# x and the histories ahead of the modulation weights, the modulation split between the projections, the norm rows made during out_b

## The reference

```
mod = silu(c) @ w_ada + b_ada                      # (9, 6*1024): shift1, scale1, gate1, shift2, scale2, gate2
u = x * (1 + scale1) + shift1
b_g, c_g, xa, xp, g_a, g_b = split(u @ w_in)       # w_in: 1024 x 4096
zc = concat(conv_hist, c_g * xa);  conv = sum_j conv_w[j] * zc[:, j:j+T]
y_a = (b_g * conv) @ w_out_a
diff = multiscale_pool(concat(pool_hist, xp))
y_b = (einsum(diff, w_pool) * ls_pool) @ w_out_b
merged = sigmoid(g_a) * y_a + sigmoid(g_b) * y_b
h = layer_norm(ALPHA * x + gate1 * (merged @ w_o), ln1_g, ln1_b)
v = h * (1 + scale2) + shift2
f = moe_ffn(v)                                     # router, top 4 of 32, SwiGLU experts
y = layer_norm(ALPHA * h + gate2 * f, ln2_g, ln2_b)
```

## Time and profile before

| | |
|---|---|
| three runs | 1304.96, 1297.54, 1305.26 us; median 1304.96 |
| the profiled execution | 1306.29 us, its span 1304.5 us |
| PE busy | 1202.6 us (92%) |
| DVE, ACT, POOL busy | 550.4, 226.6, 160.6 us |
| DMA | 466.54 MB, mean 358 GB/s over the span |

### The profile page before, as it was taken

The page is one execution under the profiler, slowest core; times in us unless marked ns, Lnnn a source line. Parts: engine busy times, 40 slices in busy tenths (PEclk is TensorE's granted clock), DMA queues, the critical chain, the costliest instruction groups (busy, mean ns, idle before and its releaser), DMA issues.

```text
span 1304.5 us, 17407 instructions
## 1 busy us (share of the span) xinstructions
PE 1202.6 (92%) x6170; PEld 520.2 (40%) x6171; DVE 550.4 (42%) x1044; ACT 226.6 (17%) x350; POOL 160.6 (12%) x97
## 2 busy tenths in 40 slices
PE   4899999979899999999899999999999999999990
PEld 0599964433333333333333333333333333333330
DVE  0517825874434333433334333443343433334337
ACT  0233210133112111111111111111111111111110
POOL 0367443024400000000000000000000000000023
PEclk8799999969899999999999999999999999999995
DMA  9744499649999999999996999998899999699951
GB/s 335 261 153 173 193 310 369 245 183 400 394 425 428 426 427 427 426 426 425 425 426 255 427 425 426 426 428 356 333 426 428 427 427 426 263 425 426 426 237 40
DMA packets 54789, 466.54 MB, mean 358 GB/s; under 512 B 5516, under 2 KB 5548, under 8 KB 18642
## 3 DMA queue, kind: packets, MB, share of 16 engines
q1 hardware_dynamic: 52817, 460.32, 85.9%
q0 software_dynamic: 1952, 5.97, 1.4%
HBM read 464.42 MB, written 1.85 MB: 357 GB/s over the span
## 4 chain that ended last, share of the span: by engine, by line
PE 60%; DMA 27%; DVE 9%; SPq 2%; ACT 1%; issue 1%; POOL 0%; DVEq 0%; ACTq 0%
PE bank L870 28%; DMA ring<-in_w_up 21%; PE bank L904 13%; PE bank L647 8%; PE bank L844 3%; DMA mod_rows<-parts_home 3%; DMA hx<-in_x_sample 2%; PE bank L767 2%; PE bank L633 2%; DVE front L1354 1%; PE bank L895 1%; ACT front L1038 1%; DVE front L1348 1%; PE bank L862 1%; DVE front L1345 1%
## 5 line engine op out<-in xcount | busy, mean ns | idle before, releaser
L870 PE MATMUL bank<-ring,front 128*64 128x512 f32 x2240 | 505.9, 597 | 20.3 <-DMA ring<-in_w_up 20.3
L870 PEld LDWEIGHTS bank<-ring,front 128*64 128x64 f32 x2240 | 153.5, 137 | 314.7 <-issue 269.8
L904 PE MATMUL bank<-ring,front 128*64 128x512 f32 x1120 | 250.2, 599 | 7.1 <-ACT front L1038 7.1
L1328 DVE TENSOR_TENSOR front<-front,bank 128x512 f32<-128x512 f32 (+1 forms) x210 | 143.7, 684 | 78.7 <-PE bank L844 65.9
L904 PEld LDWEIGHTS bank<-ring,front 128*64 128x64 f32 x1120 | 77.8, 138 | 155.5 <-issue 141.6
L1371 DVE TENSOR_TENSOR O_low<-bank,O_high 128x512 fp32r<-128x512 f32 x35 | 24.2, 691 | 247.0 <-ACT O_high L1041 247.0
L1035 ACT ACTIVATE front<-front 128x256 f32<-128x256 f32 x70 | 29.2, 417 | 529.0 <-DVE front L1345 529.0
L549 POOL TENSOR_TENSOR parts_home<-front 128x1024 f32<-128x1024 f32 (+1 forms) x2 | 4.7, 2356 | 919.9 <-DVE onehot_T L1368 919.9
L1345 DVE TENSOR_SCALAR front<-bank 128x256 f32<-128x256 f32 x70 | 29.7, 424 | 159.8 <-PE bank L870 158.6
L467 POOL TENSOR_TENSOR ring_parts<-ring,ring_parts 128x1024 fp32r<-128x1024 f32 x28 | 68.3, 2472 | 77.2 <-ACT ring_parts L937 77.2
L767 PE MATMUL bank<-parts_home,front 128*64 128x512 bf16 (+1 forms) x560 | 70.5, 382 | 0.0
(11 more groups left out here) (217 smaller groups left out, 938.6 us busy)
## 6 DMA issues: line engine op xcount, KB each, us to landing
ring<-in_w_up SPq DMA_DIRECT2D x128, 2048.0 KB, 18.3
ring<-in_w_down SPq DMA_DIRECT2D x128, 1024.0 KB, 17.4
ring<-in_w_ada SPq DMA_DIRECT2D x12, 2048.0 KB, 16.0
ring<-in_w_in SPq DMA_DIRECT2D x8, 2048.0 KB, 11.9
ring<-in_w_o SPq DMA_DIRECT2D x2, 2048.0 KB, 19.6
hx<-in_x_prompt SPq DMA_DIRECT2D x2, 1024.0 KB, 23.7
ring<-in_w_out_a SPq DMA_DIRECT2D x1, 2048.0 KB, 7.3
ring<-in_w_out_b SPq DMA_DIRECT2D x1, 2048.0 KB, 14.2
```

The costliest lines, as they stand in the source:

```text
L870: last = mm(bank[B_UP[j]][64 * h:64 * h + 64, :], x_T[:, (c % 2) * 2 + b, 64 * (c // 2):64 * (c // 2) + 64], w[:, :, at:at + 256], start=F ...
L904: last = mm(bank[B_DOWN][64 * h:64 * h + 64, :], act_T[:, 2 * j + b, 64 * hh:64 * hh + 64], expert_chunk_at(UP_CHUNKS + m)[:, b * 1024 + h ...
L1328: signal(TT(Y[0:r, 2 * t + h, :], Y[0:r, 2 * t + h, :], bank[b][0:r, :], ALU.add), bank_free[b], value)
```

## The change

- SP loads x ahead of the first chunk of w_ada and the two histories ahead of the second; b_ada comes as four rows instead of four copies of nine.
- The bias of a modulation third is a product of a selection matrix (`mod_sel`, new in the constants) with the bias rows, the first into the third's bank; for the first third a row of ones adds the 1 of 1 + scale1. VectorE's additions become a copy (the other two thirds: a copy by ScalarE).
- TensorE transposes x and the histories before `ada(0)`. ScalarE copies the transposed x to SBUF; later ScalarE makes u of the prompt in place (`Identity` with scale and bias), VectorE that of the samples.
- The eight chunks of thirds 1 and 2 go one by one through ring slot 1, and TensorE takes one behind each projection. Projections use seven PSUM banks, the eighth is kept for the thirds.
- `gain_and_offset` is called in VectorE's drain of out_b, ahead of blocks 2 and 5; the wait for the norm rows moves ahead of the drain of out_a.
- SP: third 0 is no longer stored; w_o's first half is asked for ahead of x's second load, its second half behind the rows. Ring slots of rows and experts change accordingly.

The core of the diff:

```diff
-FRONT_SLOT = (0, 1, 2, 3) + (4, 5, 0, 1, 4, 5, 0, 1) + (4, 5, 0, 2) + (1, 3) + (4, 5, 0, 2) + (1, 4)
+ADA_N = ((0, 1, 2, 3), (7, 9, 11, 13), (15, 17, 19, 21))
+IN_N = (4, 5, 6, 8, 10, 12, 14, 16)
+OUTA_N, OUTB_N = 18, 20
+O_N = (22, 23)
+FRONT_SLOT = (0, 1, 2, 3, 4, 5, 0, 1, 4, 1, 5, 1, 0, 1, 4, 1, 5, 1, 0, 1, 4, 1, 2, 3)
-ROW_SLOT = (5, 0)
-EXPERT_SLOT = (2, 3, 1, 4, 5, 0)
+ROW_SLOT = (5, 1)
+EXPERT_SLOT = (0, 4, 2, 3, 5, 1)
...
+            x_rows_in()
+            ada_chunk(0, 0)
+            sp.wait_ge(ones_ready, 1)
+            sp.dma_start(b_ada_rows[0:4, :, :], a["b_ada"][0].rearrange("(n q m) -> q n m", n=3, q=4)).then_inc(bada_landed, 16)
+            sp.dma_start(conv_hist[0:NSEQ * HIST_C, :], a["state_conv"][0].rearrange("s t d -> (s t) d")).then_inc(hist_landed, 16)
+            sp.dma_start(pool_hist[0:NSEQ * HIST_P, :], a["state_pool"][0].rearrange("s t d -> (s t) d")).then_inc(hist_landed, 16)
+            for i in (1, 2, 3):
+                ada_chunk(0, i)
+            in_chunk(0)
+            in_chunk(1)
+            in_chunk(2)
+            ada_chunk(1, 0)
+            for i in (3, 4, 5):
+                in_chunk(i)
+                ada_chunk(1, i - 2)
+            in_chunk(6)
+            ada_chunk(2, 0)
+            store_mod(1)
+            in_chunk(7)
+            ada_chunk(2, 1)
+            front_chunk(OUTA_N, a["w_out_a"][0].rearrange("(k p) n -> p k n", p=P), (4, D))
+            ada_chunk(2, 2)
+            front_chunk(OUTB_N, a["w_out_b"][0].rearrange("(k p) n -> p k n", p=P), (4, D))
+            ada_chunk(2, 3)
...
+            o_chunk(0)
             wait_full(sp, LAST_PROJ)
+            x_rows_in()
...
             mod_for_tokens(2 * D, 4 * D, norm1_landed, norm1_landed)
+            o_chunk(1)
             store_mod(2)
-            sp.wait_ge(mod_stored, 16 * 12)
+            sp.wait_ge(mod_stored, 16 * 8)
             mod_for_tokens(4 * D, 5 * D, scale2_landed[0], scale2_landed[1])
...
+            def ada(third, i):
+
+                ps = take(f"ada{third}") if i == 0 else bank[front_place(f"ada{third}")[0]]
+                if i == 0:
+                    n = 5 if third == 0 else 4
+                    mm(ps[:, :], mod_sel[0:n, :], b_ada_rows[0:n, third, :], start=True, stop=False)
...
             proj_plain(IN_ORDER[0])
...
+            ada(1, 0)
             for i in range(1, 8):
                 proj(i, IN_ORDER[i])
+                ada(*divmod(i + 4, 4))
...
-            ada(1)
             pe.wait_ge(conv_ready, 4)
...
-            out("out_b", w_out_b, yg_T, range(4))
-            ada(2)
-            out("out_b", w_out_b, yg_T, range(4, 8))
+            out("out_b", chunk(OUTB_N).rearrange("p (k m) -> p k m", k=4), yg_T, range(8))
...
+            for k in range(KC):
+                q, blk = divmod(k, 4)
+                wait_read(act, f"x_T{k}")
+                AF(u_T[:, k, 0:NP_TOK], u_T[:, k, 0:NP_TOK], ACT.Identity, bias=mod_T[:, blk, 32 * q:32 * q + 1],
+                   scale=mod_T[:, blk, 32 * q + 64:32 * q + 65]).then_inc(u_prompt_ready, 1)
...
-            ada(1)
...
+            dve.wait_ge(norm1_landed, 16 * (3 + NSEQ))
             for m in range(KC):
                 ps = wait_full(dve, f"out_a{m}")
...
             for m in range(KC):
-                if m == 4:
-                    ada(2)
+                if m in (2, 5):
+                    gain_and_offset(m // 4)
                 ps = wait_full(dve, f"out_b{m}")
                 wait_read(dve, f"proj{24 + m}")
                 step(TT(gb_T[:, m, :], gb_T[:, m, :], ps[:, 0:NT], ALU.mult))
...
             residual(0, 0)
-            gain_and_offset(0)
             residual(0, 1)
             v_rows(0)
-            gain_and_offset(1)
```

More of the change, by code:

```diff
@@ L625, in _ @@
                 done(f"x_T{k}", last)
+            pe.wait_ge(hist_landed, 32)
+            for name, src, r in (("conv_hist_T", conv_hist, 16), ("pool_hist_T", pool_hist, 120)):
+                ps = take(name)
+                for blk in range(4):
+                    last = nc.tensor.transpose(ps[:, blk * r:(blk + 1) * r], src[0:r, blk * P:(blk + 1) * P], ident[0:r, 0:r])
+                done(name, last)
+            wait_read(pe, "c_T")
+            pe.wait_ge(bada_landed, 16)
+            for i in range(4):
+                ada(0, i)
+            wait_read(pe, "ada0")
+            ps = take("mod_T")
+            for blk in range(4):
+                last = nc.tensor.transpose(ps[:, blk * P:(blk + 1) * P], mod[:, 0, blk * P:(blk + 1) * P], ident)
+            done("mod_T", last)
             def proj_plain(m4):
-                w = chunk(IN_CHUNK).rearrange("p (k m) -> p k m", k=KC)
+                w = chunk(IN_N[0]).rearrange("p (k m) -> p k m", k=KC)
                 blocks = [take(f"proj{4 * m4 + j}") for j in range(4)]
                 for k in range(KC):
-                    wait_read(pe, f"x_T{k}")
+                    pe.wait_ge(u_prompt_ready, k + 1)
+                    pe.wait_ge(u_sample_ready, k + 1)
                     for j in range(4):
@@ L820, in _ @@
             last.then_inc(bank_full[B_X], 1)
-            wait_read(pe, FRONT[[n for n in range(len(FRONT)) if n % 8 == B_XT][-1]])
+            wait_read(pe, in_bank(B_XT)[-1])
             x_transposes(0)
@@ L1082, in _ @@
             free("chan_T", v.tensor_copy(chan, ps[:, 0:16]))
-            dve.wait_ge(bada_landed, 64)
-            def ada(third):
-                ps = wait_full(dve, f"ada{third}")
-                for q in range(4):
-                    r = slice(32 * q, 32 * q + NC_ROWS)
-                    ins = TT(mod[r, third, :], ps[r, :], b_ada_rows[r, third, :], ALU.add)
-                    if q < 3:
-                        step(ins)
-                    else:
-                        free(f"ada{third}", ins)
```

225 lines of the change are left out of this document (104 added, 121 removed).

## The result

The changed kernel takes 1309.66 us (median of 20 runs, 1303.83 to 1314.55), the kernel before 1304.83 on the same chip (20 runs, 1297.54 to 1309.0): a ratio of 1.0036, 95% interval 1.0024 to 1.0048. It is slower by 4.8 us, 0.4%. It lies within 1% and inside the range, as forecast; but the measurement tells the two kernels apart, to the slow side, and the forecast of 1304.6 was 5.1 us short. The execution profiled took 1313.09 us (span 1311.3), 3.4 above its median (that of the kernel before stands 1.5 above its own), so the traces show some 2 us more of a difference than the medians.

The account below looks back on a forecast made before the run. The prediction took TensorE to bound the front and weight transfers the expert loop. Terms -7.0 + 9.0 - 2.4 = -0.4 us took the profiled 1306.29 to 1305.9; the median, 1.3 lower, gave 1304.6 us, range 1291 to 1315.

Parts of the forecast that it names:

- -7.0: Front through the last w_o product: it would end at 248.3 against 255.26, 7.0 us earlier if TensorE never waits.
- +9.0: Out_b drain: TensorE's added wait for VectorE at the w_o products, 9 us, bounds 6.5 and 12.
- -2.4: Tail, last w_o product to last v tile: 7.2 us instead of 9.6, so 2.4 us less.
- TensorE waits 9 us: W_o products: norm operations in out_b's drain take turns with GpSimd's up-bias preparation, so block 7 comes 9 us late.
- nearly neutral: Moving the two modulation thirds between the projections: 15.8 us in, 17.1 us out, as TensorE was full on both sides.
- the chunk now arrives about when x did: Start: last chunk of the first modulation third, behind x and histories, at 35.3, or 33.1 without the dent.
- The dent at 22 to 24 us: Start of the kernel before: slow transfers, 2.2 us lost in 4, put down to the nine-fold bias load.
- +39 of S: Out_b drain: first three norm operations end 39 us after S, the end of the state transposes, expected at 178.7.
- No wait of VectorE for `mod_rows`: Tail: VectorE no longer waits for modulation rows from DRAM, where it waited 8.64 and 2.38 us before.
- GpSimd always first: Out_b drain: VectorE stands until +38.5, a wait of 13 us, time 1308.6; a tenth of the forecast's 0.55 chance.
- Of the rivals, the first: No wait at out_b: the 9 us stay away, -9.4 us, 1295.6; chance 0.30, about half of it under 1292.

Follow-up runs that it names:

- e8: Changed kernel with three quarters of the old nine-fold bias load (162 KB, read by nobody) put back behind the new one: 1312.37 us.
- e10: Changed kernel with the histories loaded behind the first two projection chunks and transposed behind the first projection, x still in front: 1307.25 us.
- e11: Changed kernel with norm rows in the tail, up-bias early, the drain's product in PSUM and histories behind the first two projection chunks: 1298.38 us.
- e9: Changed kernel with each modulation piece behind projections 2 to 8 cut in two, its first half between that projection's second and third pass: 1336.62 us.
- e2: Changed kernel with GpSimd loading and preparing the up-bias before the out_b drain, norm operations left in that drain: 1298.68 us.
- e1: Changed kernel with the norm operations (`gain_and_offset`) moved back from the out_b drain to VectorE's tail: 1300.53 us.
- e5: Kernel before, without the change, with GpSimd's up-bias loaded and prepared early as in e2: 1299.17 us, ratio 0.9959.
- e4: Changed kernel with the edits of e1 and e2 together, norm operations in the tail and up-bias early: 1299.07 us.
- e7: Changed kernel with norm operations back in the tail and the out_b drain's product written into PSUM, up-bias preparation left beside the drain: 1296.69 us.

## Why the prediction was wrong

It forecast -0.4 us as the sum of -7.0, +9.0 and -2.4, and called that no change. The terms were of the right kind; three were mis-sized, all to the same side, and the sign went with them. The last v tile was forecast at 264.5 and came at 271.50, 7.0 us later. By the prediction's own steps that is +1.6 from the start, -0.8 from the first projection, +2.5 from the projection stage, -0.3 from out_a and out_b, +4.6 from the w_o products with their wait, and -0.6 from the tail. The step that failed most is "TensorE waits 9 us": the wait was priced at its length alone, and the lower clock behind it, 5.5 us, was put at nothing (the wait itself was 1.0 us shorter than forecast). The others are "nearly neutral" for the move of the thirds, which cost 2.5 us, and "the chunk now arrives about when x did".

- **The start: 4.7 us promised, 3.1 found** (40.0 against 41.64). Here "the chunk now arrives about when x did" has 5.8 us for x and nothing for the histories, although these too had moved ahead of three of the four chunks. The chunk was to land at 33.1 and was used at 35.23. The dent at 22 to 24 us is likely the bias load, as the prediction inferred (e8: 2.1 us); the histories made a new one (e10, e11: 2.2 us). Without them the first projection starts at 36.1 and 38.8, in part because x was early there. The other seven traces with this start have it between 40.24 and 42.52 (e8 apart), all above the forecast 40.0. The projection itself kept its length (19.8 against 20.5).
- **The projection stage: 114.2 us forecast, 116.7 measured.** No gaps, as said. But the pieces were priced as in a long row (7.05 for four). Between projections a piece takes 1.83 (62.44 to 64.27), a projection 14.28 (64.27 to 78.55) instead of 14.06, and a bias product of two records 1.05 (61.39 to 62.44) instead of 0.87. Eight times 0.07, seven times 0.22 and two times 0.18 make the 2.5 us. e9 shows the same kind of price, 0.23 a place. What was called "nearly neutral" cost TensorE at each place where the operands change.
- **States, out_a and out_b: right** (4.0 and 34.5 against 4.0 and 34.8).
- **The new wait: place, cause and length right, its price too small.** The first norm group was to end at +39 of S: it ended at 219.16, +37. That it came so close is partly luck: GpSimd began at 202.00, +19.9 instead of +17.5, and the blocks ahead of the norm operations waited less than assumed (block 0 ended at +22.1, not +24). The drain was to end at +50 and ended at 233.45, +51.3; the waits were to be 9 us and are 8.04. But the w_o part took 48.4 us, 13.7 more than the 34.7 of e2, and the prediction had 34.8 + 9.0. The rest of it is TensorE's clock (windows as above, clock in the third column from the end):

```profile
220.00:222.00 2.00, 0.00 (x0) 0.00 (x0) 2.00 (x1) 0.00 (x0) 2.00 (x1) 0.62 0.99 426
222.00:224.00 2.00, 0.52 (x1) 0.50 (x2) 1.93 (x3) 0.00 (x0) 1.94 (x2) 0.50 0.66 283
...
234.00:236.00 2.00, 2.00 (x4) 0.83 (x3) 0.00 (x0) 0.00 (x0) 0.00 (x0) 0.50 0.00 0
...
238.00:240.00 2.00, 2.00 (x6) 0.93 (x5) 1.15 (x2) 0.00 (x0) 0.00 (x0) 1.00 0.00 0
```

  In the wait the granted clock falls from 1.00 to 0.50, 1.2 GHz, and after each wait TensorE works on at it for some us: 6 records in 4.92 us and 22 in 12.74, where 32 took 13.90 in e2. That is 2.3 and 3.2 us, 5.5 in all, and with the 8.04 of waiting the 13.7 to within 0.2. The prediction counted the wait and let the products behind it run at full clock; for the first projection it had taken the clock into its bounds, here not. In e1, with waits of 0.43 and 0.97 us, the granted clock stayed at 1.00.
- **The tail: the number right, the reason half.** 6.56 us against 7.2 forecast and 9.61 before. With the norm operations back in the tail it is 6.57 (e1), so the early rows shortened it and not the move of the operations. "No wait of VectorE for `mod_rows`" held for the tail alone: the 12.72 us ahead of out_a's drain were not foreseen, and cost TensorE nothing.
- **The order of turns: right.** "GpSimd always first" fell: VectorE got an operation after each of GpSimd's. The prediction took the order of issue to speak for that rival; in the rows of the drain it gives the turns, since the blocked VectorE operation had started ahead of GpSimd's next one.
- **What it didn't see in the kernel before:** VectorE's chain from the modulation rows on, 30.6 us without a pause, set the last v tile there, and the arrival of a DMA set that chain (e5). The prediction took the tail as 9.6 us behind TensorE's last w_o product. The number was right; the reading was not.

Of the rivals, the first is what e1, e2, e4 and e7 give when the wait is taken away: 1296.7 to 1300.5 us, the prediction had 1295.6. The change without its norm rows in the drain is faster than before, by 0.4%; with them, slower by 0.4%.

## What to carry to other kernels

Before work is moved into a stretch, list for that stretch what GpSimd does there and which VectorE operations have both inputs in SBUF; where they met here they took turns, and writing one operand of the drain's operations into a PSUM bank that is free anyway removed it. Price every transfer that is moved ahead of a critical one, the small ones too. A wait of TensorE can cost more than its length, when the granted clock falls in it and comes back only some us later; and a full stage paid some 0.2 us here at each place where two kinds of products alternate. Before work is moved out of a tail, find out what sets that tail: here it was the arrival of rows, and the move gained nothing.

## What the runs showed of the hardware

- Waits of 1.5 to 3.4 us cost two thirds as much again. In e9 the stage took 206.90 - 60.61 = 146.3 us instead of 116.7, 29.6 more, of which 16.9 are waits and 7 x 0.23 = 1.6 the extra places; of the other 11, 10.1 stand in five passes and five half pieces behind a wait that took longer than their like (the pass at 96.15 took 6.73 instead of 4.96 us); behind the other two waits, of 1.47 and 2.05 us, the products kept their length. The window of that pass's start, clock in the third column from the end:

```profile
94.30:97.00 2.70, 2.68 (x11) 0.98 (x12) 0.00 (x0) 0.00 (x0) 0.00 (x0) 0.50 0.00 0
```

- The place of one operand decides the lock: VectorE's addition beside the same GpSimd subtraction took 3.72 us with both inputs in SBUF (e1) and 0.49 with one in PSUM (e7). The Trainium skill, "SBUF — State Buffer", section "Who interferes with whom", states that a VectorE instruction with at most one SBUF input, outside the two-port modes, does not contend with GpSimd. The trace agrees.
- 272 KB of histories held up a 2 MB chunk by 2.2 us, about three times what their bytes would take at 400 GB/s; 162 KB of a bias read nine-fold held it up by 2.1 us (2.7 counted from x) in one execution, about five times. That the short rows are the reason was not tested.
